# Expert weights loaded two strips at a time, and a feed-forward stage computed by seven products instead of eight

## The reference

```python
# first block: experts (16 of them, 32 tokens each, hidden width 2048)
xe = h[bidx, idx]                                   # 32 chosen tokens per expert
a = jnp.einsum('becd,edf->becf', xe, w_gate)        # w_gate, w_up: 16 x 1024 x 2048
b = jnp.einsum('becd,edf->becf', xe, w_up)
ye = jnp.einsum('becf,efd->becd', jax.nn.silu(a) * b, w_down)   # 16 x 2048 x 1024
return jnp.zeros_like(h).at[bidx, idx].add(ye * gates[..., None])

# second block: dense feed-forward, D_FF = 2816
h = rmsnorm(x, g_pre_ffn[l])
gu = h @ w_ffn_in[l]                                # 256 x 1024 times 1024 x 5632
gate, up = gu[..., :D_FF], gu[..., D_FF:]
x = x + rmsnorm((jax.nn.silu(gate) * up) @ w_ffn_down[l], g_post_ffn[l])
```

## Time and profile before

| | |
|---|---|
| median of 3 runs | 1777.16 us (1776.64 to 1779.48) |
| profiled execution, its own time | 1774.88 us |
| span of its core | 1773.1 us |
| PE busy | 1419.3 us, 80% |
| PE weight loads | 769.1 us, 43% |
| DVE busy | 324.1 us, 18% |
| ACT busy | 187.7 us, 11% |
| bytes moved by DMA | 517.66 MB |
| mean granted clock of TensorE | 0.91 |

### The profile page before, as it was taken

The page is one execution under the profiler, slowest core; times in us unless marked ns, Lnnn a source line. Parts: engine busy times, 40 slices in busy tenths (PEclk is TensorE's granted clock), DMA queues, the critical chain, the costliest instruction groups (busy, mean ns, idle before and its releaser), DMA issues.

```text
span 1773.1 us, 19596 instructions
## 1 busy us (share of the span) xinstructions
PE 1419.3 (80%) x7856; PEld 769.1 (43%) x7856; DVE 324.1 (18%) x798; ACT 187.7 (11%) x509; POOL 34.6 (2%) x96
## 2 busy tenths in 40 slices
PE   8978656766666567666666679999999999999998
PEld 5533111211121112111211126878777888677775
DVE  2442001200110011011001112345334101200001
ACT  2221000000000000000000001133223000100000
POOL 1100000000000000000000000000000000000000
PEclk9999888887887888878888879999999999999999
DMA  9668999999999999999999992123130336034431
GB/s 402 242 250 354 427 427 431 426 428 428 428 428 427 428 429 426 428 428 428 429 427 429 427 429 103 64 107 109 50 157 24 152 144 262 35 123 172 173 148 48
DMA packets 41112, 517.66 MB, mean 292 GB/s; under 512 B 4592, under 2 KB 5616, under 8 KB 8048
## 3 DMA queue, kind: packets, MB, share of 16 engines
q1 hardware_dynamic: 39152, 513.98, 69.4%
q10 hardware_dynamic: 1920, 3.11, 0.5%
HBM read 515.50 MB, written 1.05 MB: 291 GB/s over the span
## 4 chain that ended last, share of the span: by engine, by line
PE 53%; DMA 42%; DVE 2%; issue 1%; ACT 1%; SPq 0%; POOL 0%; ACTq 0%; POOLq 0%; PEldq 0%; DVEq 0%
PE ps L898 51%; DMA ring<-in_experts 42%; PE ps L1263 1%; PE ps L904 1%; DVE turned_T L1511 1%; ACT xn L770 0%; DVE scr L1623 0%; DMA vecs<-in_vecs 0%; PE ps L981 0%; ACT scr L776 0%; DVE xn L1747 0%; PE ps L957 0%; SPq L180 0%; PE ps L1357 0%; DVE scr L1591 0%
## 5 line engine op out<-in xcount | busy, mean ns | idle before, releaser
L898 PE MATMUL ps<-ring,scr 128*32 128x512 f32 (+1 forms) x3200 | 549.4, 744 | 260.7 <-DMA ring<-in_experts 245.5
L898 PEld LDWEIGHTS ps<-ring,scr 128*32 128x32 f32 (+1 forms) x3200 | 130.3, 128 | 638.8 <-DMA ring<-in_experts 400.3
L898 PE MATMUL ps<-turned_T,ring 128*128 128x256 f32 (+2 forms) x1984 | 384.4, 363 | 7.3 <-PE ps L898 3.1
L898 PEld LDWEIGHTS ps<-turned_T,ring 128*128 128x128 f32 (+1 forms) x1984 | 334.5, 186 | 57.9 <-issue 14.7
L898 PE MATMUL ps<-scr 128*128 128x512 f32 (+10 forms) x640 | 158.8, 406 | 19.5 <-DVE scr L1623 13.0
L898 PE MATMUL ps<-ring,turned_T 128*128 128x128 f32 (+3 forms) x640 | 170.8, 425 | 2.3 <-DVE turned_T L1511 1.5
L898 PEld LDWEIGHTS ps<-ring,turned_T 128*128 128x128 f32 x640 | 106.3, 190 | 64.4 <-issue 49.0
L898 PEld LDWEIGHTS ps<-scr 64*128 64x128 f32 (+4 forms) x640 | 83.2, 173 | 95.5 <-issue 51.4
L1626 DVE TENSOR_TENSOR x<-x,ps 128x512 f32<-128x512 f32 x64 | 44.0, 687 | 261.2 <-PE ps L898 261.2
L1618 DVE SCALAR_TENSOR_TENSOR scr<-scr,ps 128x512 f32<-128x512 f32 x16 | 11.0, 688 | 279.5 <-PE ps L898 279.5
L1616 DVE SCALAR_TENSOR_TENSOR scr<-scr,ps 128x512 f32<-128x512 f32 x16 | 11.0, 688 | 198.9 <-ACT scr L691 198.9
(11 more groups left out here) (243 smaller groups left out, 631.1 us busy)
## 6 DMA issues: line engine op xcount, KB each, us to landing
ring<-in_experts SPq DMA_DIRECT2D x188, 2048.0 KB, 24.6
ring<-in_w_ffn_in SPq DMA_DIRECT2D x11, 2048.0 KB, 9.1
ring<-in_w_merge SPq DMA_DIRECT2D x8, 1536.0 KB, 6.4
ring<-in_w_ffn_down SPq DMA_DIRECT2D x11, 1024.0 KB, 4.8
ring<-in_w_out SPq DMA_DIRECT2D x4, 2048.0 KB, 23.7
ring<-in_w_ml SPq DMA_DIRECT2D x4, 2048.0 KB, 7.8
ring<-in_w_nsa SPq DMA_DIRECT2D x4, 2048.0 KB, 7.7
ring<-in_w_proj SPq DMA_DIRECT2D x8, 1024.0 KB, 6.1
```

The source lines that it names most:

```text
L898: return pe.matmul(o, l, rr, start=start, stop=stop)
```

## The change

It has two parts.

**Expert strips in pairs.** On the host two neighbouring strips of an expert are laid side by side, so that a row is 32 KB. For experts 1 to 15, strips 0 to 9 are loaded as five pairs of 4 MB (`load_two`) into two neighbouring slots; it waits until both are free, and the full count of the first slot announces both. Strips 10 and 11 stay single. The slots are the same for every expert (`ROT` is 2), since `w_ple_proj` and the `w_mem_kv` strips leave the ring for slot 9, an area in `scr`. SP issues them inside the list of the first expert of a part: `w_ple_proj` after expert 1's first two pairs, once expert 0's h exists, and a `w_mem_kv` strip behind that expert.

**Feed-forward by block products.** Each product of two by two blocks is formed by seven block products and a set of sums before and after (the Winograd form of Strassen's scheme). In `ff_in` the blocks are halves of the contraction (k 0 to 3 and 4 to 7), gate against up, and halves of the tokens; a product has 8 matmuls of 128 columns, so a step has 56 where it had 32 of 256. DVE forms four sums of the weights for each step (`sums_in`, four instructions of 1024 elements a partition), and once four sums of the activations (`tT`). After the products it combines seven half banks in eight instructions of 256 elements (`total` and a copy), and only then come tanh and h. `w_ffn_down` is repacked so that strip n holds the blocks n and n + 11 of the 22 blocks of 128 hidden units. All h is kept (`hF`), and the down products are computed after the eleventh step: 11 times seven matmuls of 512 columns into seven banks, with `sums_down` before each and eight combining instructions of 512 elements at the end.

```diff
-ROTS = [3, 4, 5, 0]
...
+ROT = 2
+PAIRED = {0: (2, 2), 1: (2, 1), 2: (2, 2), 3: (2, 0), 4: (2, 2), 5: (2, 0)}
...
+    def load_two(self, slot, dst, src):
+        for s in (slot, slot + 1):
...
+            self.eng.wait_ge(self.free[s], r)
...
+        self.eng.dma_start(dst, src).then_inc(self.full[slot], 16)
+        self.count(slot, 1)
+        self.count(slot + 1, 0)
...
+            def paired(e, slots, embed=False):
+                for n in range(0, 10, 2):
+                    if embed and n == 4:
+                        sp.wait_ge(h_sb, 1)
+                        sp.dma_start(*whole(9, "w_ple_proj", 0)).then_inc(full[9], 16)
+                    s = slots[n]
+                    r.load_two(s, ring[:, s * SLOT:(s + 2) * SLOT], packed["experts"][bass.ds((e * 6 + n // 2) * P, P), :])
+                for n in (10, 11):
+                    r.load(slots[n], strip_of(slots[n], e, n))
+            def experts(part, rot, first=0):
+                n = PARTS[part] - first
+                with sp.Fori(0, n) as i:
+                    r.enter(i, PAIRED)
+                    paired(i + sum(PARTS[:part]) + first, around(rot))
+                    r.leave(n)
+            def with_aside(part, quarter):
+                paired(sum(PARTS[:part]), around(ROT), quarter == 0)
+                if quarter:
+                    sp.wait_ge(mkv_ps, quarter)
+                else:
+                    sp.wait_ge(e_ps, 4)
+                sp.dma_start(*whole(9, "w_mem_kv", quarter)).then_inc(full[9], 16)
+                experts(part, ROT, 1)
             expert(0, FIRST_SLOTS, FIRST_LOADS)
-            r.load(2, whole(2, "w_ple_proj", 0))
             for n in range(4):
-                experts(1 + n, ROTS[n])
-                r.load(ROTS[n], whole(ROTS[n], "w_mem_kv", n))
...
+                with_aside(1 + n, n)
...
-            def ff(s, par):
+            def ff_in(s, par):
                 r.load(2 + 2 * par, whole(2 + 2 * par, "w_ffn_in", s, tslot))
-                r.load(3 + 2 * par, whole(3 + 2 * par, "w_ffn_down", s, tslot))
...
+            def ff_down(k):
+                r.load(DOWN[k % 4], whole(DOWN[k % 4], "w_ffn_down", k, tslot))
+            ff_in(0, 0)
+            ff_in(1, 1)
+            ff_down(0)
+            ff_down(1)
             with sp.Fori(0, 4) as i:
...
+                ff_in(i * 2 + 2, 0)
+                ff_in(i * 2 + 3, 1)
                 r.leave(4)
...
+            ff_in(10, 0)
+            for k in range(2, HALF):
+                ff_down(k)
...
-            wple = slot[2][:, 0:2 * D].rearrange("p (k n) -> p k n", k=2)
+            pe.wait_ge(full[9], 32)
...
             def ff_in(s, par):
+                a, b = par * 4, hT.rearrange("p (j k) (t n) -> p j t k n", j=2, t=NT)
+                w = tstrip[2 + 2 * par].rearrange("p (j k) (i n) -> p j i k n", j=2, i=2)
+                sums = sF[1 - par]
+                half = lambda q: bank[4 - 4 * par + q // 2][:, (q % 2) * T:(q % 2 + 1) * T]
                 r.arrived(2 + 2 * par, 1)
-                for f in range(2):
...
-            def ff_down(s, par, first=False, last=False):
...
+                if par == 0 or not isinstance(s, int):
+                    pe.wait_ge(ff_h, s * 2 - 2)
...
+                for q, (l, rr) in enumerate(((w[:, 0, 0], b[:, 0, 0]), (w[:, 1, 0], b[:, 1, 0]),
+                                             (sums[:, 1], tT[:, 1]), (sums[:, 0], tT[:, 0]), (sums[:, 3], b[:, 1, 1]),
+                                             (sums[:, 2], tT[:, 2]), (w[:, 1, 1], tT[:, 3]))):
+                    if q == 2:
+                        pe.wait_ge(ff_sum, s + 1)
...
+                    for f in range(2):
+                        for k in range(4):
+                            ins = mm(half(q)[:, f * P:(f + 1) * P], l[:, k, f * P:(f + 1) * P], rr[:, k, :], k == 0, k == 3)
+                            if (q, f, k) == (0, 0, 0):
+                                ins.then_inc(tfree[4 - 2 * par], 1)
+                    if q in (1, 3, 5, 6):
...
+            def ff_down(n):
+                s = DOWN[n % 4]
+                w = tslot[s][:, 0:2 * D].rearrange("p (j i n) -> p j i n", j=2, i=2)
+                a = [[hF[:, c // 2, t, c % 2, :] for c in (n, n + HALF)] for t in range(NT)]
+                ss, tt = sD[(n + 2) % 3], tD[(n + 2) % 3]
+                r.arrived(s, 1)
+                for q, (l, rr) in enumerate(((a[0][0], w[:, 0, 0]), (a[0][1], w[:, 1, 0]), (ss[:, 1], tt[:, 1]),
+                                             (ss[:, 0], tt[:, 0]), (ss[:, 3], w[:, 1, 1]), (ss[:, 2], tt[:, 2]),
+                                             (a[1][1], tt[:, 3]))):
+                    if q == 2:
+                        pe.wait_ge(ff_sum, 12 + n)
+                    if n == 0 and q in (0, 4):
+                        pe.wait_ge(ff_h, 2 * FF_STEPS - 2 + q // 2)
+                    ins = mm(bank[q], l, rr, n == 0, n == HALF - 1)
+                    if q == 0:
+                        ins.then_inc(tfree[DOWN[(n - 1) % 4]], 1)
+                    if q == 6 or n == HALF - 1 and q in (1, 4, 5):
                         ins.then_inc(ffo_ps, 1)
-                    elif k == 0 and t == 0 and h == 0:
-                        ins.then_inc(tfree[4 - 2 * par], 1)
-                if not last:
-                    ins.then_inc(tfree[3 + 2 * par], 1)
...
-            pe.wait_ge(ff_ps, 2)
-            pe.sem_inc(tfree[2], 1)
             ff_in(1, 1)
-            ff_down(0, 0, first=True)
             with pe.Fori(0, 4) as i:
...
                 ff_in(i * 2 + 2, 0)
-                ff_down(i * 2 + 1, 1)
                 ff_in(i * 2 + 3, 1)
-                ff_down(i * 2 + 2, 0)
                 r.leave(4)
             ff_in(10, 0)
-            ff_down(9, 1)
-            ff_down(10, 0, last=True)
+            for n in range(HALF):
+                ff_down(n)
...
+            def sums_in(s, par):
+                w = tstrip[2 + 2 * par].rearrange("p (j k) (i n) -> p j i k n", j=2, i=2)
+                o = sF[1 - par]
+                dve.wait_ge(tfull[2 + 2 * par], s * 8 + (8 if par else 16) + landed[2 + 2 * par])
+                chain(dve.tensor_tensor(o[:, 0], w[:, 0, 1], w[:, 1, 1], ALU.add))
+                sub(o[:, 1], o[:, 0], w[:, 0, 0])
+                sub(o[:, 2], w[:, 0, 0], w[:, 0, 1])
+                dve.tensor_tensor(o[:, 3], w[:, 1, 0], o[:, 1], ALU.subtract).then_inc(ff_sum, 1)
+            def sums_down(n):
+                s = DOWN[n % 4]
...
+                w = tslot[s][:, 0:2 * D].rearrange("p (j i n) -> p j i n", j=2, i=2)
+                a = [[hF[:, c // 2, t, c % 2, :] for c in (n, n + HALF)] for t in range(NT)]
+                ss, tt = sD[(n + 2) % 3], tD[(n + 2) % 3]
+                if n > 2:
+                    dve.wait_ge(ffo_ps, n - 2)
+                dve.wait_ge(tfull[s], landed[s] + 16 * (used + n // 4 + 1))
+                chain(dve.tensor_tensor(ss[:, 0], a[1][0], a[1][1], ALU.add))
+                sub(ss[:, 1], ss[:, 0], a[0][0])
+                sub(ss[:, 2], a[0][0], a[1][0])
+                sub(ss[:, 3], a[0][1], ss[:, 1])
+                sub(tt[:, 0], w[:, 0, 1], w[:, 0, 0])
+                sub(tt[:, 1], w[:, 1, 1], tt[:, 0])
+                sub(tt[:, 2], w[:, 1, 1], w[:, 0, 1])
+                dve.tensor_tensor(tt[:, 3], w[:, 1, 0], tt[:, 1], ALU.subtract).then_inc(ff_sum, 1)
...
+            def ff_in(s, par, h):
+                half = lambda q: bank[4 - 4 * par + q // 2][:, (q % 2) * T:(q % 2 + 1) * T].rearrange("p (f n) -> p f n", f=2)
+                dve.wait_ge(ff_ps, s * 4 - 1)
+                chain(dve.tensor_copy(u3F, half(0)))
+                total(gF[:, 0], half(1), u3F)
+                dve.wait_ge(ff_ps, s * 4)
+                total(u2F, half(2), u3F)
+                total(u3F, half(3), u2F)
+                dve.wait_ge(ff_ps, s * 4 + 1)
+                total(gF[:, 1], half(4), u3F, ff_h)
+                total(u2F, half(5), u2F)
+                total(uF[:, 1], half(3), u2F)
+                dve.wait_ge(ff_ps, s * 4 + 2)
+                total(uF[:, 0], half(6), u2F)
+                if h is not None:
+                    h()
+                dve.wait_ge(ff_th, s + 2)
+                chain(dve.scalar_tensor_tensor(out=gF, in0=thF, scalar=1.0, in1=gF, op0=ALU.add, op1=ALU.mult))
+                dst = hF[:, s] if isinstance(s, int) else hF.rearrange("p s t f n -> p s (t f n)")[:, bass.ds(s, 1), :]\
...
+                dve.scalar_tensor_tensor(out=dst, in0=gF, scalar=0.5, in1=uF, op0=ALU.mult, op1=ALU.mult).then_inc(ff_h, 1)
             with dve.Fori(0, 4) as i:
-                chain.enter(i, 4)
...
+                chain.enter(i, 2 * (7 + 3 + 1))
+                for par in (1, 0):
+                    s = i * 2 + 2 - par
+                    ff_in(s, par, lambda: sums_in(s + 2, par))
                 chain.leave(4)
...
+            sums_down(0)
...
+            sums_down(1)
+            ff_in(10, 0, None)
+            for n in range(2, HALF):
+                sums_down(n)
```

(14 more changed lines are left out.)

173 lines of the change are left out of this document (95 added, 78 removed).

## The result

| | median, us | runs |
|---|---|---|
| before | 1776.45 | 1774.12 to 1779.69 (20) |
| after | 1782.62 | 1777.67 to 1787.15 (20) |

The ratio after to before is 1.0028, with a 95% interval of 1.0021 to 1.0035: 5.0 us slower (3.7 to 6.2); the medians are 6.2 us apart. The forecast was slower, 1785 in a range of 1770 to 1799. The profiled execution of after has a span of 1778.8 us, that of before 1773.1.

A forecast was written before the change was run, and what follows sets the result against it. Experts were taken as bound by the weight stream, feed-forward by PE until something else is later. Experts +3.2 and feed-forward +4.7 sum to +7.9: 1782.8 against the profiled 1774.88, 1785 against the median; range 1770 to 1799.

The forecast's parts named there:

- Rows of 32 KB: Experts' weight stream: 75 pairs replace 150 strips, same bytes in half the packets; -3 us, between -9.4 and +8.7.
- the far end of 9.4: Experts: best-case saving of long rows, 14 ns a packet over 75 pairs, 9.4 us.
- The place of w_ple_proj: Experts 0 and 1: PE waits for the later w_ple_proj, frees slots late, the queue runs dry; +5.5 us, bounds 3 to 8.
- The last pair: End of the experts: pair (8,9) begins when strip 9 lands, not strip 8; +0.7 us.
- PE's own work: Feed-forward: steps of 12.7 us and cheaper down products save PE 20.6 us in all, if it never waits.
- The added wait: Feed-forward: chain of matmul, issue, load, sums and h takes 15.1 us a step, so PE waits 2.3; stage +1.2 us.
- The end: After PE's last matmul: DVE finishes combining and four halves, ending at +8.5 us instead of 4.95; +3.5 us.
- The first rival: Feed-forward steps run at PE's pace, load and sums taking 2.4 us less; in all -11.3 us, 1766; 8%.
- The second: Experts: long rows pay and the queue does not run dry, -7.3 to -4.3 us; in all about -1, 1776; 20%.
- the third: Stream slower for good at 423 GB/s, in all +19.6 us, 1797, or PE's clock falls in the 2.3 us waits; 18%.

The follow-up runs named there:

- the feed-forward kernel: Only the feed-forward part of the change, with the experts of before; 1780.36 us, ratio 1.0019 to before.
- the chain broken: Feed-forward part of the change alone, experts of before, with DVE's sums for strip s + 2 moved behind h of step s; 1758.91 us, ratio 0.9908 to before.

## Why the prediction was right, step by step

The sum was +7.9 us; the measured difference is 5.0 (3.7 to 6.2). The mechanisms are the ones named, on the right side; sizes were off in both halves. That the experts came out near the forecast (+3.2, measured 1.7) is in part luck: the gain of the rows was 2.8 us larger than I had it and the loss by the gap 2.3 us larger, and the two errors nearly cancel. The feed-forward stage was put at +4.7 and came to 3.0 in after, and to 1.5 to 2.7 in four other kernels with the same code there.

- *Rows of 32 KB, -3.* Mis-sized: -5.8 by the kernel with rows of 16 KB and twice the DMAs. I cut the far end of 9.4 to a third because a DMA share of 1.01 seemed to say that a cost per packet is hidden; it did not hide most of it. Here the estimate by the Trainium skill (DMA: Bandwidth & Descriptors, Where 436 GB/s comes from), -6 from its ceiling of 435.2 GB/s, was the better one; the mean of the stage stays under that ceiling, at 431.
- *The place of w_ple_proj, +5.5.* Right in kind, too small: 7.8. From the issue of strip 10, I had PE start the product after 36.1 us (175.3 - 139.2); it did after 37.5 (179.00 - 141.48). The wait was 6.9 and came to 7.31. The larger part is the clock: the product took 2.5 us longer than before, where I had allowed one or two for all of PE's idle time, inside the bounds of 3 to 8.
- *The last pair, +0.7.* Not seen: 921.86 - 5.8 + 7.8 = 923.9 without it, and 923.6 was measured. The column scatters by 0.3, so this says little against a term of that size.
- *PE's own work.* A step of 12.7 and a down product of 0.859 stand as worked out: 12.74, and from 1705.51 to 1768.43 62.9 us for 73 products, 0.862 each.
- *The added wait.* Chain 15.1 (its parts add up to 15.03), measured 15.1 in after and 15.0 in the feed-forward kernel; every part of it came as the rows had said (landing 7.7, sums 1.22 and 1.23, h 0.69 twice), among them the instruction of 128x1024 that no row of before showed. From the 1544.24 of before and the 1546.99 of after, where the second half of the first products begins, to PE's last end it is 221.46 and 221.44: +0.0 where I had +1.2, since the wait behind step 10 was 1.65 us and not 2.7. In the feed-forward kernel the same stretch is 219.98: its steps are 0.1 us shorter each, and it begins its second step 0.5 us earlier. So this term lies between 0 and -1.5.
- *The end, +3.5.* DVE ends 7.93 us behind PE in place of 4.95: +3.0.
- *What I did not reckon with* is the size of what no part of the change causes: 2.3 us before strip 10, and -1.3 in the middle. One profiled execution of each is no measure of 1 us.

The first rival (the step at PE's pace) was not what happened, but its price was near: with the chain broken the stage takes 17 us less, where the rival had 19.2 for the steps. The second (long rows pay and no gap) is just what the kernel with `w_ple_proj` behind one pair does: 6 us less in the experts, where it had 4.3 to 7.3. Of the third, the steady slower stream is refuted (431 GB/s). Its other half, that the clock falls in the waits between steps, is where my reasoning failed: I expected it to hold, and it fell in some of them. Behind an idle of 2.39 us 32 matmuls took 3.81, which is the spacing of 0.113 us; behind one of 2.42 us 112 took 14.37 in place of 12.74. The forecast did not suffer, because the start of the next step is set by DVE's chain and the lost 1.6 us come out of its wait.

## What to carry to other kernels

When an operation is taken off the busiest engine by giving another engine work before it, write down the chain from the start of one step to the start of the next before counting operations: here DVE was idle for a third of each step and PE for up to 2.4 us too, because sums that nobody needed yet stood ahead of an h that PE waited for. A side load in a saturated queue is not priced by its bytes but by who waits for it and which buffers that engine then frees late; try its place one load earlier and one later. And cut each execution into stages by marks in the trace before comparing: a difference of 5 us in 1780 was half hidden under 2 to 5 us before strip 10 and in the middle, which the changed code did not cause as far as these runs show.
